# Sixteen experts in fourteen units ordered by token count, in a two-layer diffusion backbone

## What is computed

```python
idx = top_k(where(in_group, sigmoid(h @ w_router) + b_router, NEG_INF), 2)
gates = one_hot(idx) * w / sum(w)
hid = silu(h @ w1[e]) * (h @ w3[e])          # 1024 -> 256, for every expert e
out = sum over e of (hid * gates[e]) @ w2[e] # 256 -> 1024
x = x + gate2 * out
```

## Time and profile before

| | us |
|---|---|
| median of 3 runs | 1189.07 |
| lowest and highest | 1189.02, 1189.97 |
| the profiled execution | 1190.82 |
| its span, first to last instruction | 1189.2 |

### The profile page before, as it was taken

One profiled execution on the slowest core, in us unless ns is written; L12 is line 12 of the kernel. 1 busy time (PEld: TensorE's weight loads), 2 busy tenths in 40 slices (PEclk: granted clock), 3 DMA queues, 4 the chain that ended last, 5 costly groups with the idle time before them and its releaser, 6 DMA issues.

```text
span 1189.2 us, 13631 instructions
## 1 busy us (share of the span) xinstructions
PE 1121.5 (94%) x4356; PEld 604.3 (51%) x4356; DVE 536.3 (45%) x1275; ACT 282.8 (24%) x653; POOL 208.8 (18%) x288
## 2 busy tenths in 40 slices
PE   5999999998999999999799999989899879999995
PEld 3556766554444454444355676745544435444442
DVE  1146543874237433433441545477623644333326
ACT  2121222663011211111141112156601111111111
POOL 5026101010115100000463410000112230000022
PEclk9999999999999999999999999999999999999998
DMA  9577822893207899998865941178300589999954
GB/s 350 209 245 289 315 109 92 349 370 145 107 26 279 323 386 366 368 367 302 322 231 154 388 149 36 43 293 337 107 18 0 189 343 354 359 373 371 358 176 196
DMA packets 63318, 291.17 MB, mean 245 GB/s; under 512 B 9504, under 2 KB 10672, under 8 KB 47328
## 3 DMA queue, kind: packets, MB, share of 16 engines
q1 hardware_dynamic: 33344, 190.87, 42.8%
q0 software_dynamic: 22720, 78.75, 18.6%
q10 hardware_dynamic: 7200, 20.87, 4.4%
HBM read 240.06 MB, written 56.98 MB: 250 GB/s over the span
## 4 chain that ended last, share of the span: by engine, by line
PE 84%; DVE 6%; DMA 4%; issue 2%; ACT 2%; POOL 1%; SPq 0%; ACTq 0%; POOLq 0%; DVEq 0%
PE ps L1235 13%; PE ps L1536 12%; PE ps L1715 9%; PE ps L1693 9%; PE ps L1696 9%; PE ps L1170 3%; PE ps L1163 3%; PE ps L1470 2%; PE ps L1501 2%; PE ps L1481 2%; PE ps L1146 2%; PE ps L1749 2%; DMA expert_in<-arena,pos_i 2%; PE ps L1145 2%; PE ps L1101 2%
## 5 line engine op out<-in xcount | busy, mean ns | idle before, releaser
L1235 PE MATMUL ps<-arena 128*128 128x320 f32 x560 | 156.6, 432 | 0.0
L1536 PE MATMUL ps<-arena 128*128 128x512 f32 x320 | 140.4, 594 | 2.4 <-issue 2.4
L1235 PEld LDWEIGHTS ps<-arena 128*128 128x128 f32 x560 | 105.0, 190 | 42.6 <-issue 1.0
L1715 PE MATMUL ps<-arena 128*128 128x512 f32 x256 | 115.4, 594 | 3.7 <-issue 3.7
L1693 PE MATMUL ps<-arena 128*128 128x512 f32 x256 | 117.2, 601 | 1.3 <-DVE arena L2791 1.3
L1696 PE MATMUL ps<-arena 128*128 128x512 f32 x256 | 115.1, 592 | 0.0
L2791 DVE COPY arena<-ps 128x512 f32<-128x512 f32 x32 | 22.1, 691 | 203.3 <-PE ps L1676 203.3
L1536 PEld LDWEIGHTS ps<-arena 128*128 128x128 f32 x320 | 59.5, 190 | 74.6 <-issue 74.6
L1693 PEld LDWEIGHTS ps<-arena 128*128 128x128 f32 x256 | 48.9, 192 | 62.5 <-issue 60.4
L1696 PEld LDWEIGHTS ps<-arena 128*128 128x128 f32 x256 | 48.6, 190 | 61.2 <-issue 61.2
L1715 PEld LDWEIGHTS ps<-arena 128*128 128x128 f32 x256 | 46.1, 190 | 50.5 <-issue 50.5
(11 more groups left out here) (332 smaller groups left out, 1652.2 us busy)
## 6 DMA issues: line engine op xcount, KB each, us to landing
arena<-in_w SPq DMA_DIRECT2D x96, 1024.0 KB, 9.3
arena<-in_w_ada SPq DMA_DIRECT2D x40, 1024.0 KB, 6.8
expert_in<-arena POOLq DMA_DIRECT2D x2, 8192.0 KB, 33.4
expert_out<-arena ACTq DMA_DIRECT2D x30, 512.0 KB, 8.1
arena<-expert_in POOLq DMA_DIRECT2D x28, 512.0 KB, 9.7
arena<-in_w_t SPq DMA_DIRECT2D x10, 1024.0 KB, 10.6
arena<-in_w_ada_c SPq DMA_DIRECT2D x8, 1024.0 KB, 13.2
arena<-in_w_out SPq DMA_DIRECT2D x8, 1024.0 KB, 6.1
```

The source lines that it names most:

```text
L1235: ins = mm(out[:, 0:HALF], lhs[:, k, :], rhs[:, k, :], start=(first and k == 0), stop=(last and k == 3), skip_group_check=True)
L1536: ins = mm(out[:, n * 512:(n + 1) * 512], yT[:, k, t * P:(t + 1) * P], w[k // 2][:, k % 2, n * 512:(n + 1) * 512], start=(k == 0), stop=(k ...
L1715: ins = mm(out[:, n * 512:(n + 1) * 512], hidT[:, f, :], w[:, f, n * 512:(n + 1) * 512], start=(f == 0), stop=(f == 1))
```

## The change

The 14 experts 2 to 15 are ordered by their token counts; the place in this order is a role, from 2 (fewest) to 15 (most). Roles 0 and 1 stay experts 0 and 1. VectorE writes the experts of the roles to `roles_i`, from which SyncE and GpSimd load registers. Roles 2 to 9 are capped at 96 rows and packed into six units: units 2, 3 and 4 hold roles 2, 3 and 4 in rows 0 to 95, and role 5 in rows 96 to 127 in three parts of 32; units 5, 6 and 7 do the same with roles 6, 7, 8 and 9. Roles 10 to 15 have units 8 to 13 of 128 rows. If more than six of the experts 2 to 15 have more than 96 tokens, a further round is run.

In a shared unit the up and down products are written in tiles of 32 columns, three for the first role and one for the second, so four matmuls stand where one stood. The tokens are read, and the results written, in two DMAs (96 and 32 rows). All loops over units are written out.

The weights have four places for up and four for down. The two new ones lie over `h2` and the buffers of the mixing sub-layer behind it (`at_h`, `at_y`) and over small buffers at `at_up`. SyncE loads roles in the order 0, 1, 2, 5, 3, 4, 6, 9, 7, 8, 10 to 15; each role's up weights are followed by its down weights. Before role 2 it waits for the roles, for the rows picked for unit 0 and for the scatter. At the start of the kernel the rows 96 to 127 of eight roles in `expert_out` are set to zero.

```diff
+def expert_units():
+    units = [[(0, 0, P, 0)], [(1, 0, P, 0)]]
+    for low in (2, 6):
+        units += [[(low + i, 0, LOW_CAP, 0), (low + 3, LOW_CAP, P - LOW_CAP, (P - LOW_CAP) * i)] for i in range(3)]
+    return units + [[(role, 0, P, 0)] for role in range(LAST_LOW, NE)]
+PLACE_OF = {0: 0, 1: 1, 2: 2, 5: 3, 3: 0, 4: 1, 6: 2, 9: 0, 7: 1, 8: 3, 10: 2, 11: 1, 12: 3, 13: 2, 14: 0, 15: 1}
+        up_at = [at_ring + SLOT, at_ring + 3 * SLOT, at_h + 2 * SLOT, at_h]
+        down_at = [at_ring, at_ring + 5 * SLOT, at_h + 4 * SLOT, at_up]
...
 SyncE
-                    load_up(2, 0, 0)
-                        load_up(sp.snap(pair, min_val=0, max_val=NE - 2) + 1, 1, 1)
-                        load_down(sp.snap(pair, min_val=0, max_val=NE - 2), 0, 0)
+                    wait(sp, roles_ready.sem, roles_ready.at(l, 1))
+                    filled(sp, l, "tokens0")
+                    wait(sp, scattered.sem, scattered.at(l, 16 * 2 * TT))
+                        for role in LOAD_ORDER[2:-2]:
+                            q = PLACE_OF[role]
+                            e = sp.value_load(roles_i[0:1, role:role + 1], min_val=0, max_val=NE - 1)
+                            free = used_by(base, role)
+                            load_up(e, q, base + 2 if free is None else free)
+                            load_down(e, q, base + 2 if free is None else free)
...
 GpSimd
-            pool.dma_start(hs[:, b, :], slots_in(e, r)).then_inc(hs_in[b], 16)
+                            for role, lo, n, skipped in EXPERT_UNITS[u]:
+                                e = pool.value_load(roles_i[0:1, role:role + 1], min_val=0, max_val=NE - 1)
+                                src = slots_in(e, r) if n == P else some_slots_in(e, r, skipped, n)
+                                pool.dma_start(hs[lo:lo + n, b, :], src).then_inc(hs_in[b], 16)
...
 TensorE, up (down alike)
-                    for k in range(4):
-                        mm(out, hsT[b][:, k, :], w[:, k, :], start=(k == 0), stop=False)
+                    for k in range(KD):
+                        if k == 4:
+                            pe.wait_ge(hsT_high, base + u + 1)
+                        for lo, n, role in columns_of_unit(u):
+                            ins = mm(out[lo:lo + n, :], hsT[b][:, k, lo:lo + n], w[role][:, k, :], start=(k == 0), stop=(k == KD - 1),
+                                     skip_group_check=True)
...
 VectorE, behind the totals of the router
+                dve.tensor_scalar(r_over, total, float(LOW_CAP), None, ALU.is_gt)
+                dve.scalar_tensor_tensor(out=r_key, in0=total, scalar=float(NE), in1=count16, op0=ALU.mult, op1=ALU.add)
+                link(V(r_pair, per_column(keys), per_row(keys), ALU.is_ge))
+                link(dve.tensor_reduce(r_up[:, 2:NE], r_pair, AX.X, ALU.add))
...
+                link(V(r_pair, per_column(r_up[:, 2:NE]), per_row(names), ALU.is_equal))
+                link(V(r_pair, r_pair, per_column(names), ALU.mult))
+                link(dve.tensor_reduce(r_over[:, 2:NE], r_pair, AX.X, ALU.add))
+                dve.tensor_scalar(roles_i[:, 2:NE], r_over[:, 2:NE], -1.0, float(NE), ALU.mult, ALU.add).then_inc(roles_ready.sem, 1)
...
+                    link(V(r_t, r_sel, of_expert.unsqueeze(1).unsqueeze(1).broadcast_to((P, 2, TT, NE)), ALU.mult))
+                    link(dve.tensor_reduce(of_choice, r_t, AX.X, ALU.add))
```

More of the change, by code:

```diff
@@ L35 @@
 CREDIT = 2
-DVE_CHAIN = 160
+DVE_CHAIN = 171
 ROUNDS = N_TOK // P
@@ L262, with before_unit, of_round @@
 EDGES = [0, NE - 1]
+LOW_CAP = 96
+LOW_ROLES = 8
+FIRST_LOW, LAST_LOW = 2, 2 + LOW_ROLES
+def expert_units():
[3 more added lines that the diff above has]
+    return units + [[(role, 0, P, 0)] for role in range(LAST_LOW, NE)]
+EXPERT_UNITS = expert_units()
+UN = len(EXPERT_UNITS)
+PLACE_OF = {0: 0, 1: 1, 2: 2, 5: 3, 3: 0, 4: 1, 6: 2, 9: 0, 7: 1, 8: 3, 10: 2, 11: 1, 12: 3, 13: 2, 14: 0, 15: 1}
+LOAD_ORDER = list(PLACE_OF)
+LAST_UNIT = {role: max(u for u, parts in enumerate(EXPERT_UNITS) for part in parts if part[0] == role) for role in range(NE)}
+LOADS_OF = [[role for role in LOAD_ORDER if PLACE_OF[role] == q] for q in range(4)]
+ROWS_IN = [16 * len(parts) if u >= 2 else 0 for u, parts in enumerate(EXPERT_UNITS)]
+ROWS_OUT = [16 * len(parts) if u + 1 < UN else 0 for u, parts in enumerate(EXPERT_UNITS)]
+def before_unit(counts, u):
+    return sum(counts[u % 2:u:2])
+def of_round(counts, b):
+    return sum(counts[b::2])
 def mixer_kernel(nc, A, O):
@@ L1714, in down @@
                         for f in range(2):
-                            ins = mm(out[:, n * 512:(n + 1) * 512], hidT[:, f, :], w[:, f, n * 512:(n + 1) * 512],
-                                     start=(f == 0), stop=(f == 1))
+                            for lo, rows_of, role in columns_of_unit(u):
+                                ins = mm(out[lo:lo + rows_of, n * 512:(n + 1) * 512], hidT[:, f, lo:lo + rows_of],
+                                         w[role][:, f, n * 512:(n + 1) * 512], start=(f == 0), stop=(f == 1), skip_group_check=True)
                     ins.then_inc(dn_full, 1)
@@ L2854, in rounds @@
                         hidden(base, 0, 0)
-                        with dve.Fori(0, NE // 2 - 1) as i:
-                            step(2 * i + 1, 1)
-                            step(2 * i + 2, 0)
-                        hidden(base, NE - 1, 1)
-                        output(base, NE - 2, 0)
-                        output(base, NE - 1, 1)
+                        for u in range(1, UN - 1):
+                            step(u, u % 2)
+                        hidden(base, UN - 1, 1)
+                        output(base, turn, UN - 2, 0)
+                        output(base, turn, UN - 1, 1)
                         dve.wait_ge(gate2_in, turn * 32 + 32)
```

297 lines of the change are left out of this document (181 added, 116 removed).

## The result

The changed kernel is slower: 1202.93 us, the median of four executions from 1196.48 to 1205.92, against 1189.52 us for the kernel before, run beside it. The ratio is 1.0101, with a 95% interval of 1.0067 to 1.0136. The forecast was 1167.6 us. The profiled execution is the fastest, the one of 1196.48 us (span 1194.1), so the trace accounts for 5 us of the loss; the median lies 6.5 us above it.

The account below looks back on a forecast made before the run. Two limits at almost the same height: TensorE and nearly full DMAs. Of TensorE's 43.6 us saving, half turns into waiting for weights; gains of 9.8 and 11.7 us, together 21.5, take 1189.07 to 1167.6 us, range 1152 to 1181.

Parts of the forecast that it names:

- I take the DMA side as nearly full: Expert stage before the change: 366 to 368 GB/s at busy share 0.99 was read as leaving at most 1% room.
- T0: When SyncE's wait for the token scatter before role 2 ends; forecast 395.0 us in layer 0, 967.5 in layer 1.
- TensorE's saving, 21.8 us a layer: Expert stage: two of sixteen units removed save 22.8 us, entering and leaving tiled form costs 1.0; 43.6 us in all.
- Rivals D and E: D: tiles' weight loads no longer hidden, 1271 us, chance 0.08; E: second round, over 100 us per layer, chance 0.03.
- Unit 2 at T0 + 23.3: Start of the first shared unit, set by the arrival of 8.1 MB at 380 GB/s plus 2 us.
- Unit 7 at T0 + 86.2: Start of the last shared unit, set by 32.0 MB at 380 GB/s plus 2 us; 5.2 us behind TensorE's rhythm.
- A hole of 0 to 3 us per layer; I take 0: Weight queue: role 7's down load waits for unit 4's down product; counted as nothing since other queues fill part.
- Split reads "nothing; at worst the smaller parts lower the rate to the 343 end": Shared units' reads and writes in 96 and 32 rows: only more issues, no cost; at worst 343 GB/s.
- Zeros "nothing, at worst 3": Kernel start: the extra 1 MB of zeros takes 3 us of DMA time away from any TensorE wait.
- VectorE's chain, 5.4 us, hidden: Before the expert stage: some 19 new instructions delay unit 0 by up to 4 us, covered by later waits.
- "Weights are later than that": Longer gaps likely cost another 2 us of slower clock, but the next weights arrive later, so it is covered.
- Rival C: Weight supply in the expert stage is worse than 380 GB/s: at 358, gains 4.6 and 6.5, 1178.0 us; chance 0.20.

Follow-up runs that it names:

- the kernel with three causes taken away: Changed kernel with shared units' tokens read in one 128-row DMA (some wrong tokens), up weights first in the queue, and zeros written later: 1169.86 us, ratio 0.9804.

## Why the prediction was wrong, step by step

Three terms of the sum were put at nothing and were not: the split reads (1.6%), the hole in the weight queue (1.0%) and the zeros (0.4%). Together they are about 36 us, and the kernel came out 35.3 us above the forecast.

- **"I take the DMA side as nearly full": wrong.** The row read was right and the inference wrong. Being always busy is also what a queue shows that is asked for just under its capacity; 512 KB more per expert took it to 417 at no cost that can be measured. That the kernel with three causes taken away comes near the forecast (1169.86 and 1167.6 us) is in part luck. Its queues carry 418 in the shared stretch, and at that rate the prediction's own sum gives unit 7 at about T0 + 79 (the weights at 32.0/0.418 + 2 = T0 + 78.6). With T0 = 947.67 + 9.02 = 956.7 in layer 1 it starts at 1043.08, T0 + 86.4, where T0 + 86.2 was forecast with 380: waits of 4.1 and 1.2 us at units 3 and 6, and the slower product behind the first, made up for the rate that was set too low. The last up product comes at 1112.28, T0 + 155.6 (forecast: T0 + 154.9).
- **TensorE's saving, 21.8 us a layer: right** (21.8 and 22.1), with four tiles as cheap as one matmul. Rivals D and E fell.
- **Unit 2 at T0 + 23.3: right in layer 0**, T0 + 22.9 (T0 is 398.2, when the read of unit 1's tokens, which waits for the scatter, is issued), and late in layer 1, T0 + 29.0 (T0 is 969.3).
- **Unit 7 at T0 + 86.2: wrong**, T0 + 97.1 and T0 + 100.5. The 380 GB/s looked right (378), but as a mean of 420 and dips below 320.
- **"A hole of 0 to 3 us per layer; I take 0": failed.** Place and cause were right, the size was not. The slices from 470 to 490 us show shares of 0.35 and 0.74, together 9.1 us of DMA time not used, and layer 1 has another of 7.2 us (shares of 0.95 and 0.33 from 1040 to 1060). I took a block behind a stalled unit as a delay of its own length. It is a loop: the weights come late, so the product that would free the place comes late, so the queue stands still, and the next weights are late. The queue order is worth 1.0%.
- **Split reads "nothing; at worst the smaller parts lower the rate to the 343 end": the step that failed most.** I priced the issues, not what narrow DMAs do to the others. They are worth 1.6%, more than the 1.0% by which the changed kernel is slower.
- **Zeros "nothing, at worst 3": wrong.** TensorE waits 2.5 to 3.7 us for what comes behind them in every trace that has them at the start, and in five of these eight the slower clock behind the wait adds 1.7 to 3.1 us. In the trace of the changed kernel the clock holds, and everything from 117 us on is 3 us later, T0 of layer 0 with it.
- **VectorE's chain, 5.4 us, hidden: size right** (from 386.39 to 391.5), hidden in this kernel. Unit 0 starts at 397.81 instead of 390.20; 3 us of it are the zeros, and the other 4.6 answer to the "up to 4" of the prediction (4.9 in the kernel with late zeros). Where weights are no problem it shows: in the kernel with half the up weights unit 2 starts at 422.2, no earlier than here.
- **"Weights are later than that" for the slow clock: wrong.** The clock falls in the wait for the weights themselves, and the product behind it pays 2.3 to 2.8 us. No later wait covers this: unit 3 of layer 1 starts without one.
- **Rival C's premise** (358, with the page's figure) has the wrong mechanism for both kernels: 417 GB/s were carried for 126 us on end. The Trainium skill, DMA: Bandwidth & Descriptors, section "Where 436 GB/s comes from", has about 358 GB/s as the bound for transfers between HBM and SBUF. These 417 GB/s, loads and writes of results together, contradict it as a ceiling for this core.
- **The range** ended at 1181 because no case had the hole, the dips or the clock behind the zeros in it. With only the dips gone the time was 1182 us, with only the hole gone 1188 us.

## What to carry to other kernels

A DMA share near 1 doesn't tell a full queue from a well fed one: add traffic and see. In a queue that blocks on buffers, put what is needed first and free first ahead of what waits for the newest work, and price a blocked queue by how long its head waits, not by how long the consumer does. Where the queues are full, read in DMAs that span all partitions, even if there are two of them; the kernels that did so here had the wrong tokens in rows 96 to 127, so a version of this change that gains by it and is right is still to be found. A wait of 3 us can cost 6 where the clock drops behind it.

## What the runs showed of the hardware

- A DMA into 96 or 32 of 128 partitions beside large loads lowered the total rate from about 419 to between 275 and 341 GB/s for 3 to 4 us, with the DMA engines as busy as before. With two DMAs of 128 partitions and 2 KB a row, one window of 2 us in both stretches together was that low; with the same rows in parts of 96 and 32 it was 24. By what mechanism is open.
- One core's queues carried 416 to 418 GB/s over 50 to 126 us.
- Behind a wait of TensorE of 2.5 to 3.7 us at 117 us the granted clock stayed at 1.00 in three traces and was 0.65 to 0.82 from 118.5 to 128 us in five, with the same matmuls behind it (11.03 us, or 12.7 to 14.1). Behind waits for weights of over 6 us, products of 7.07 us took 9.4 to 9.9.
- The start of unit 0 in layer 0 lay between 393.97 and 403.80 us in the profiles of the variants of the changed kernel. Most of this is the wait for what follows the zeros and the clock behind it: with both it is 401.49 to 403.80, with the wait alone 395.53 to 397.81, with neither 393.97 to 398.19. It is part of the variants' spread of up to 1%.
